# Two-block kernel on one core: the second tile's expert weights added by GpSimd into a cleared table, and a new order of the choice steps

## The chip, the cores and the metric

One core of a Trainium2 chip runs the whole program in one launch. The metric is device time in microseconds (us) for one execution. The engines are TensorE (PE), VectorE (DVE), ScalarE (ACT), GpSimd (Pool) and SyncE (SP), which issues most of the DMAs. TensorE runs at 2.4 GHz or, when the chip's gate holds it back, at 1.2 GHz; the profile gives the share granted as PEclk.

## What is computed

The reference is two transformer blocks on 512 tokens of width 1024 in float32. The first has gated delta-rule and sparse attention and an FFN; the second has gated linear attention, a state-space mixer and a PEER layer, which this case is about:

```python
q = (hb @ w_q).reshape(n, PEER_HEADS, 2, PEER_HALF)
s = jnp.einsum('nhid,hikd->nhik', q, sub_keys)
s_top, i_top = lax.top_k(s, PEER_TOPK)                 # 16 of 128, twice per head
cand = s_top[:, :, 0, :, None] + s_top[:, :, 1, None, :]
best, pos = lax.top_k(cand.reshape(n, PEER_HEADS, 256), PEER_TOPK)
w = jax.nn.softmax(best, axis=-1)
act = jax.nn.gelu(jnp.einsum('nhkd,nd->nhk', u, hb))   # u: rows of u_tab at idx
out = jnp.einsum('nhk,nhkd->nd', w * act, jnp.take(v_tab, idx, axis=0))
```

There are 8 heads, 16 picks per head (128 picks per token) and 16384 experts. An expert has a row in `u_tab` and one in `v_tab`.

## The kernel before

**Two ways to the experts.** The 512 tokens are four tiles of 128. For tile 0 the kernel fetches the 128 chosen rows of every token: a GpSimd indirect DMA brings row n of all tokens into a buffer `ub` (0.5 MB), and DVE multiplies it with the token (`gather_ve`, L3240, first 128 rows) or adds it, weighted, to `acc` (second 128 rows). For tiles 1 to 3 (ND = 384 tokens) it computes all 16384 experts densely: `u_pe` multiplies 128 tiles of `u_tab` with the tokens, ACT takes the gelu into `gst` and SP writes it to `gelu_spill`; later the v phase reads it back, multiplies it with a table of expert weights (mostly zeros) and multiplies the result with `v_tab`.

**The table of weights.** For tiles 1, 2 and 3 it is made in hot steps: a pick's expert is i * 128 + b, and for four tokens at a time DVE builds one-hot matrices `Bh` (L3027) and, with the weight, `Ah` (L3030), PE multiplies them (four matmuls of 128x128 per step), ACT copies the result into `stage` (L3011) and SP writes `stage` to `weight_spill` (`spill`, L3039), six halves of 4 MB in four DMAs of 1 MB each. One tile has 32 hot steps.

**The choice.** `top_ve(j)` makes tile j's list: for j of 2 and 3 sixteen `top16` on 128 values (for 0 and 1 these are done before this stage), then the sums of candidates, eight `top16` on 256 values, and seven passes over 2048 elements that turn places into indices, `sel`. `hot_*(j)` needs the list j, `gather_po` the list 0.

**The order.** Each engine's program is written by generators. `weave` takes a step of each in turn at given rates. `together((u_x, 1), (choose_x, CHOOSE))` weaves the dense u work (256 steps on each engine, four per 1 MB weight tile) with the choice, CHOOSE = 1.14 choice steps to one u-step. All engines use the same counts, so that their orders agree. `choose` runs top(0), top(1), then hot(1) with top(2) and 16 rows, hot(2) with top(3) and 16 rows, hot(3) with 16 rows, then 32 rows and the start of the v phase (`start_*`: SP fetches the first three pieces, DVE `weigh`s two, ACT makes the high half `ph`, DVE the low half `pl`). `top_idle` holds the place of a list on engines that have nothing to do in it, and must have as many steps.

**Weight tiles.** SP loads them into a ring of four. ACT makes the high half `wh` (L521), DVE the low half `wl` (L528), both with two buffers, and PE multiplies three times (high with high, low with high, high with low) at L573.

**Rows in flight.** `gather_po` issues row n after row n-2 is used, with two buffers, until row 48 (RT); from there with six buffers, four of which lie over `stage`.

**The first FFN** (`ffn_*`) begins with `arrive(.., 3)`; SP then loads `x1`, and DVE's `ffn_ve` waits for it, adds PE's results of the four `wout1` tiles to it and makes the `wl` of later tiles in between.

## Time and profile before

| | |
|---|---|
| median of 3 runs | 3211.97 us (3210.53 to 3214.05) |
| the profiled execution | 3215.74 us, span 3213.9 us |
| PE busy / DVE busy / ACT busy / Pool busy | 3068.6 / 2213.7 / 1152.6 / 418.7 us |
| mean granted TensorE clock | 0.967 |
| DMA | 571.10 MB, 178 GB/s over the span |
| of this: software queue (Pool's) | 134.23 MB in 36864 packets |
| chain that ended last | PE 79%, DVE 12%, DMA 4%, ACT 3% |

The span is the time from the first to the last instruction in the trace; the rest of the execution's time lies around it. A view of stretches gives the busy time of each engine between two times, with the number of instructions in brackets. In a view in order of time the bracket at the end of a row is the idle time before the instruction and who ended it. Busy spans of neighbouring instructions overlap a little, so a price is best taken from start to start. Busy PE time is not useful work as such: at half clock the same matmuls are busy twice as long.

### The profile page before, as it was taken

The numbers are of one execution on the slowest core, as the hardware profiler recorded it, in microseconds if no ns is written. First come the engines' busy times: TensorE is split into PE (matmuls) and PEld (weight loads), VectorE is DVE, ScalarE is ACT, GpSimd is POOL, SyncE is SP. The second block draws the span as 40 slices with busy tenths as digits, with TensorE's granted clock in tenths as the row PEclk, the third lists the DMA queues.
The fourth block names the chain that finished last, engine by engine and source line by source line (L and its number), as shares of the span: only waits on it lengthen the run. The fifth ranks groups of instructions, "written<-read, shape, count | busy, mean of one in ns | idle before, by whom it ended". The sixth has DMA issues, their size and how long they took to land.

```text
span 3213.9 us, 42988 instructions
## 1 busy us (share of the span) xinstructions
PE 3068.6 (95%) x17723; PEld 2809.3 (87%) x17723; DVE 2213.7 (69%) x3737; ACT 1152.6 (36%) x1569; POOL 418.7 (13%) x264
## 2 busy tenths in 40 slices
PE   7998998999999999999999999899999969999998
PEld 7887887878879889998877789899999969999998
DVE  6437875755644443567753568898998767899996
ACT  2224233222233442455543323344445522333332
POOL 0000000000000000000000000011111254565551
PEclk9889998999999998999999999899999989999999
DMA  5223112222232133212224414447777799999995
GB/s 230 88 111 146 40 53 105 75 94 100 79 125 89 67 109 133 79 53 81 86 91 164 170 66 144 154 168 233 258 235 260 268 378 352 403 402 401 402 399 216
DMA packets 215715, 571.10 MB, mean 178 GB/s; under 512 B 14289, under 2 KB 129489, under 8 KB 180065
## 3 DMA queue, kind: packets, MB, share of 16 engines
q1 hardware_dynamic: 176496, 426.14, 36.9%
q0 software_dynamic: 36864, 134.23, 10.9%
q10 hardware_dynamic: 2160, 7.99, 0.6%
q8 instruction: 140, 2.29, 0.3%
q14 instruction: 55, 0.44, 0.0%
HBM read 495.95 MB, written 72.35 MB: 177 GB/s over the span
## 4 chain that ended last, share of the span: by engine, by line
PE 79%; DVE 12%; DMA 4%; ACT 3%; SPq 1%; issue 1%; DVEq 0%; ACTq 0%
PE bank L573 71%; DMA wv<-weight_spill 3%; PE bank L1236 2%; DVE wl L528 2%; PE bank L637 2%; PE bank L2507 1%; PE bank L585 1%; PE bank L644 1%; DVE acc L148 1%; DVE Ah L3030 1%; PE bank L2516 1%; ACT wh L521 1%; PE bank L1501 0%; DVE sr L2859 0%; DMA cst<-in_consts 0%
## 5 line engine op out<-in xcount | busy, mean ns | idle before, releaser
L573 PE MATMUL bank<-hh,wh 128*128 128x512 f32 (+2 forms) x2512 | 925.1, 368 | 44.9 <-DVE wl L528 25.4
L573 PE MATMUL bank<-hl,wh 128*128 128x512 f32 (+2 forms) x2512 | 899.1, 358 | 0.0
L573 PE MATMUL bank<-hh,wl 128*128 128x512 f32 (+2 forms) x2512 | 894.1, 356 | 0.0
L528 DVE TENSOR_TENSOR wl<-ring,wh 128x2048 fp32r<-128x2048 f32 (+2 forms) x249 | 554.4, 2226 | 315.5 <-ACT wh L521 314.8
L521 ACT ACTIVATE wh<-ring 128x2048 fp32r<-128x2048 f32 (+2 forms) x249 | 463.7, 1862 | 781.2 <-PE bank L573 772.8
L573 PEld LDWEIGHTS bank<-hh,wh 128*128 128x128 f32 x2512 | 484.5, 193 | 101.5 <-DVE wl L528 28.4
L573 PEld LDWEIGHTS bank<-hl,wh 128*128 128x128 f32 x2512 | 484.8, 193 | 49.8 <-issue 6.0
L573 PEld LDWEIGHTS bank<-hh,wl 128*128 128x128 f32 x2512 | 484.3, 193 | 46.2
L3226 POOL DMA_INDIRECT ub<-in_urow,gsel x128 | 200.3, 1565 | 1452.8 <-DVE gsel L2957 885.7
L573 PE MATMUL bank<-ph,wh 128*128 128x384 f32 x1024 | 346.2, 338 | 22.0 <-DVE pl L3189 22.0
L573 PE MATMUL bank<-pl,wh 128*128 128x384 f32 x1024 | 345.3, 337 | 0.0
L573 PE MATMUL bank<-ph,wl 128*128 128x384 f32 x1024 | 345.2, 337 | 0.0
L3226 POOL DMA_INDIRECT ub<-in_vrow,gsel x128 | 216.9, 1695 | 148.2 <-DVE acc L148 115.1
L573 PEld LDWEIGHTS bank<-ph,wh 128*128 128x128 f32 x1024 | 193.5, 189 | 22.6 <-issue 20.8
L573 PEld LDWEIGHTS bank<-pl,wh 128*128 128x128 f32 x1024 | 193.5, 189 | 0.0
L573 PEld LDWEIGHTS bank<-ph,wl 128*128 128x128 f32 x1024 | 193.5, 189 | 0.0
L148 DVE SCALAR_TENSOR_TENSOR acc<-ub,gwt,acc 128x1024 f32<-128x1024 f32 x127 | 163.0, 1283 | 8.9 <-DVE acc L148 0.5
L3240 DVE SCALAR_TENSOR_TENSOR ub<-ub,hh_u 128x1024 f32<-128x1024 f32 x128 | 152.7, 1220 | 9.2 <-DMA ub<-in_urow,gsel 9.2
L573 PE MATMUL bank<-wh,hh 128*128 128x256 f32 (+2 forms) x520 | 154.3, 297 | 0.1
L573 PE MATMUL bank<-wh,hl 128*128 128x256 f32 (+2 forms) x520 | 150.8, 290 | 0.0
L573 PE MATMUL bank<-wl,hh 128*128 128x256 f32 (+2 forms) x520 | 150.8, 290 | 0.0
L1960 POOL TENSOR_TENSOR kdm<-kdm,km 128x16 f32<-128x16 f32 x4 | 1.3, 321 | 1131.9 <-ACT kdm L1927 1131.9
(515 smaller groups left out, 4456.0 us busy)
## 6 DMA issues: line engine op xcount, KB each, us to landing
ring<-in_v SPq DMA_DIRECT2D x68, 1024.0 KB, 16.2
ring<-in_u SPq DMA_DIRECT2D x64, 1024.0 KB, 5.6
ring<-in_ada SPq DMA_DIRECT2D x24, 1024.0 KB, 4.9
gelu_spill<-gst SPq DMA_DIRECT2D x128, 192.0 KB, 3.2
weight_spill<-stage SPq DMA_DIRECT2D x24, 1024.0 KB, 8.2
gv<-gelu_spill SPq DMA_DIRECT2D x64, 384.0 KB, 10.5
wv<-weight_spill SPq DMA_DIRECT2D x64, 384.0 KB, 14.5
ring<-in_wup SPq DMA_DIRECT2D x22, 1024.0 KB, 4.8
```

The lines of the kernel that those rows point to most:

```text
L148: return e.scalar_tensor_tensor(out=out, in0=a, scalar=x, in1=b, op0=op0, op1=op1)
L521: a.then_inc(a.e.activation(wh[q % 2][:, 0:n], ring[k % 4][:, 0:n], ACT.Copy), s("whi"))
L528: v.then_inc(v.e.tensor_tensor(wl[q % 2][:, 0:n], ring[k % 4][:, 0:n], wh[q % 2][:, 0:n].bitcast(F32), S_), s("parts"))
L573: ins = p.e.matmul(out, l, r, start=start and i == 0, stop=stop and i == len(pairs) - 1, skip_group_check=not check)
L585: return p.e.transpose(out, in_, ident[0:k, 0:k])
L637: ins = p.e.matmul(out[:, j:j + 1], sq[:, 128 * j:128 * j + 128], C["ones"][:, 0:1], start=start and j == 0, stop=stop, skip_group_check=True)
L644: ins = p.e.matmul(out[:, 128 * j:128 * j + 128], r[:, j:j + 1].to_broadcast([128, 128]), ident, start=j == 0, stop=True, skip_group_check ...
L1236: ins = p.e.matmul(ps[:, 128 * h:128 * h + 128], l, r, start=h == 0 and n_ == 0, stop=True, skip_group_check=True)
L2507: p.then_inc(p.e.matmul(bank[7][:, :], l, r, start=True, stop=True), s("ss_mm"))
L2516: p.then_inc(p.e.matmul(bank[6][:, :], CTm[:, q, 128 * j:128 * j + 128], SS[c % 2][:, :], start=q == 0, stop=q == 1), s("pi_mm"))
L3226: g.e.indirect_dma_start(ub[b][:, :], None, D["urow" if n < 128 else "vrow"], bass.IndirectOffsetOnAxis(gsel[:, 0, n % 128:n % 128 + 1], 0 ...
L3240: v.then_inc(v.e.scalar_tensor_tensor(out=u3, in0=u3, scalar=1.0, in1=hT, op0=M, op1=M, accum_out=dot[:, m:m + 1]), s("gd"))
```

## The change

Tile 1 no longer goes through hot steps. Its list yields `sidx`, the place of each of a token's 128 picks in a new table `weight_scatter` (64 x 2 x 128 x 128, 8 MB), and `swt`, the weights. GpSimd adds them there: 128 indirect DMAs with an add, each of 128 elements of 4 bytes, three after each gather from row 6 on. Every sixteenth waits until all earlier ones have landed. The table is cleared before by eight DMAs of 1 MB from a tile of zeros, at the start of the first FFN. `weight_spill` has four halves left, and `fetch` reads both tables.

The order of the choice is new too: rows stand beside top(1), top(2), hot(2) and hot(3), long steps are cut in two or have an empty step after them, and CHOOSE is 1.68. 88 rows, not 80, are used in the stage.

```diff
-    wd_ = nc.dram_tensor("weight_spill", (6, 64, 128, 2, 64), F32).ap()
+    wd_ = nc.dram_tensor("weight_spill", (4, 64, 128, 2, 64), F32).ap()
+    sw_ = nc.dram_tensor("weight_scatter", (64, 2, 128, 128), F32).ap()
...
         norm_ve(v, 2, x1, cc["lnmix"])
+        v.wait_ge(s("zw"), 128)
...
     def top_idle(j):
-        for _ in range((11 if j >= EARLY else 0) + 1 + 8 + 1 + 6 + 1):
+        for _ in range((19 if j >= EARLY else 0) + 1 + 16 + 1 + 12 + 1):
             yield
...
-        v.then_inc(tt(w3, w3, bc(red8[:, 1, :], 16), M), s("wsel"))
+        if j == 1:
+            v.then_inc(tt(swt.rearrange("p (h k) -> p h k", h=8), w3, bc(red8[:, 1, :], 16), M), s("wsel"))
+            v.then_inc(stt(v.e, sel[:, 0, :], sel[:, 1, :], 128.0, sel[:, 0, :], M, A_), s("ve"))
+            v.settle()
+            v.then_inc(ts(v.e, sidx, sel[:, 0, :], 128.0, M, stok[:, 0:1], A_), s("scr"))
+        else:
+            v.then_inc(tt(w3, w3, bc(red8[:, 1, :], 16), M), s("wsel"))
...
+    def cleared_po(g):
+        arrive(g, 3)
+        g.then_inc(g.e.memset(zeros[:, :], 0.0), s("zr"))
+        g.wait_ge(s("zr"), 1)
+        flat_w = sw_.rearrange("i x b t -> (i x b t)").rearrange("(p n f) -> p n f", p=128, f=2048)
+        for n in range(8):
+            g.e.dma_start(flat_w[:, n, :], zeros[:, :]).then_inc(s("zw").sem, 16)
+
+    def scatter_po(g, k):
+        cells = sw_.rearrange("i x b t -> (i x b t)").unsqueeze(1)
+        if k == 0:
+            g.wait_ge(s("zw"), 128)
+            g.wait_ge(s("wsel"), 2)
+            g.wait_ge(s("scr"), 1)
+        if k and k % 16 == 0:
+            g.wait_ge(s("scat"), 16 * k)
+        g.e.indirect_dma_start(cells, bass.IndirectOffsetOnAxis(sidx[:, k:k + 1], 0), swt[:, k:k + 1],
+                               None, compute_op=ALU.add).then_inc(s("scat").sem, 16)
...
-    ROWS = 0, 16, 32, 48, 80
+    ROWS = 0, 6, 22, 46, 70, 88
...
-        yield from top(1)
-        yield from weave((hot(1), 1), (top(2), 0.75), (rows(ROWS[0], ROWS[1]), 0.4))
-        yield from weave((hot(2), 1), (top(3), 0.75), (rows(ROWS[1], ROWS[2]), 0.4))
-        yield from weave((hot(3), 1), (rows(ROWS[2], ROWS[3]), 0.4))
-        yield from rows(ROWS[3], ROWS[4])
+        yield from weave((top(1), 1), (rows(ROWS[0], ROWS[1]), 0.2))
+        yield from weave((top(2), 1), (rows(ROWS[1], ROWS[2]), 0.33))
+        yield from weave((hot(2), 1), (top(3), 0.7), (rows(ROWS[2], ROWS[3]), 0.33))
+        yield from weave((hot(3), 1), (rows(ROWS[3], ROWS[4]), 0.33))
+        yield from rows(ROWS[4], ROWS[5])
         yield from start
...
-    CHOOSE = 1.14
+    CHOOSE = 1.68
...
         if i < 3:
-            y.wait_ge(s("ab_mm"), 96)
+            y.wait_ge(s("ab_mm"), 64)
+            y.wait_ge(s("scat"), 2048)
...
+        y.e.dma_start(ws[i % 3][:, :, :], sw_[i].rearrange("x b t -> b x t")).then_inc(s(f"gv{i % 3}").sem, 16)
...
-        g4 = gv[i % 3][:, :, :].rearrange("p x (b t) -> p x b t", b=6)
+        g3 = gv[i % 3][:, :, 0:128]
+        v.e.tensor_tensor(g3, g3, ws[i % 3][:, :, :], M)
+        g4 = gv[i % 3][:, :, 128:ND].rearrange("p x (b t) -> p x b t", b=4)
...
+            if n >= 6:
+                for k in range(3 * n - 18, min(3 * n - 15, 128)):
+                    scatter_po(g, k)
```

A hot step takes two choice steps on each engine now, a `top16` on 256 values two, and a `top16` on 128 values one (before, two of them shared a step); the counts in `top_idle`, `top_sc`, `hot_pe`, `hot_sc`, `hot_ve` and `hot_sy` follow.

Pool's queue before, whole from its last vector work on (`kdm` belongs to the gated linear attention):

```order
L1960 TENSOR_TENSOR kdm<-kdm,km 128x16 x4
L3226 DMA ub<-in_urow,gsel 128x1024 x128
L3226 DMA ub<-in_vrow,gsel 128x1024 x128
```

and after, from the clearing to the first scatters, and the end of the scatters:

```order
L2998 MEMSET zeros 128x2048
L3002 DMA weight_scatter<-zeros 128x2048 x8
L1966 ISA
L1966 TENSOR_TENSOR kdm<-kdm,km 128x16 x4
L3275 DMA ub<-in_urow,gsel 128x1024 x7
L3012 DMA weight_scatter<-cst 2097152x1 x3
L3275 DMA ub<-in_urow,gsel 128x1024
L3012 DMA weight_scatter<-cst 2097152x1 x3
L3275 DMA ub<-in_urow,gsel 128x1024
```

`cst` holds `sidx` and `swt`. From row 6 on each gather now has three scatters behind it, up to row 48.

SP's queue at the end of the stage before, where `gv` and `wv` are the first pieces of the v phase and `gst` the gelu results:

```order
L3138 DMA gelu_spill<-gst 128x384 x2
L508 DMA ring<-in_v 128x2048
L3138 DMA gelu_spill<-gst 128x384 x2
L3170 DMA gv<-gelu_spill 128x768
L3171 DMA wv<-weight_spill 128x6x128
```

and after:

```order
L3216 DMA gv<-gelu_spill 128x768
L3217 DMA wv<-weight_spill 128x4x128
L3219 DMA ws<-weight_scatter 128x2x128
L513 DMA ring<-in_v 128x2048
L3182 DMA gelu_spill<-gst 128x384 x2
L513 DMA ring<-in_v 128x2048
L3182 DMA gelu_spill<-gst 128x384 x2
```

The fetches stood behind the last gelu write; now eight gelu writes follow them.

DVE's queue at the same place before:

```order
L528 TENSOR_TENSOR wl<-ring,wh 128x2048
L3240 SCALAR_TENSOR_TENSOR ub,dot<-ub,hh_u 128x1024
L3178 TENSOR_TENSOR gv<-gv,wv 128x384 x4
L3189 TENSOR_TENSOR pl<-gv,ph 128x768 x2
```

and after:

```order
L533 TENSOR_TENSOR wl<-ring,wh 128x2048
L3224 TENSOR_TENSOR gv<-gv,ws 128x2x128
L3227 TENSOR_TENSOR gv<-gv,wv 128x256 x2
L3224 TENSOR_TENSOR gv<-gv,ws 128x2x128
L3227 TENSOR_TENSOR gv<-gv,wv 128x256 x2
L3238 TENSOR_TENSOR pl<-gv,ph 128x768
L533 TENSOR_TENSOR wl<-ring,wh 128x2048 x4
```

Four wl, two of them for the last two u tiles, now stand behind the first `weigh`.

## Rows read from the trace of the kernel before

**Rows 1.** Stretches: busy us (instructions), PE clock, DMA share, GB/s.

```profile
1955.00:2072.00 117.00, 100.07 (x527) 98.00 (x526) 108.42 (x240) 36.00 (x40) 3.96 (x2) 0.91 0.43 152
2072.00:2258.00 186.00, 181.46 (x1118) 180.54 (x1117) 170.87 (x419) 86.72 (x88) 27.76 (x16) 0.99 0.64 214
2258.00:2445.00 187.00, 183.24 (x1128) 182.60 (x1127) 172.77 (x420) 86.50 (x90) 25.95 (x16) 0.99 0.70 235
2445.00:2566.00 121.00, 120.88 (x784) 120.58 (x783) 95.16 (x203) 64.52 (x66) 21.29 (x19) 1.00 0.82 278
2566.00:2641.00 75.00, 58.98 (x312) 58.01 (x310) 48.73 (x68) 19.23 (x21) 42.63 (x29) 0.91 1.01 371
2641.00:2659.00 18.00, 0.35 (x1) 0.38 (x2) 9.07 (x13) 1.69 (x2) 6.18 (x5) 0.55 0.98 362
2659.00:3196.70 537.70, 536.19 (x3087) 535.90 (x3087) 475.99 (x487) 169.34 (x134) 289.46 (x170) 1.00 0.98 377
```

The engines stand in the order PE, PE's weight loads, DVE, ACT, Pool.

**Rows 2.** PE's waits, 1955 to 2660: total us, times, longest.

```profile
PE bank L573 <- DVE wl L528: 25.4, 10, 4.9
PE bank L573 <- ACT gst L3121: 9.3, 1, 9.3
```

**Rows 3.** ACT in order of time: gelus, without hot work and with it.

```profile
1976.59 0.49 ACT L3121 ACTIVATE gst<-bank 128x384 f32<-128x384 f32 x1 [1.88 <-PE bank L573]
...
1985.05 0.49 ACT L3121 ACTIVATE gst<-bank 128x384 f32<-128x384 f32 x1 [1.88 <-PE bank L573]
...
2178.78 0.49 ACT L3121 ACTIVATE gst<-bank 128x384 f32<-128x384 f32 x1 [1.00 <-PE bank L573]
...
2188.97 0.49 ACT L3121 ACTIVATE gst<-bank 128x384 f32<-128x384 f32 x1 [0.97 <-PE bank L573]
```

**Rows 4.** DVE in order of time: start, us, operation.

```profile
1976.70 0.43 DVE L2856 MAX8 hl_u<-s_ 128x8 f32<-128x256 f32 x1
...
1979.08 0.43 DVE L2856 MAX8 hl_u<-s_ 128x8 f32<-128x256 f32 x1
...
2185.27 0.67 DVE L3027 TENSOR_TENSOR Bh<-cst,hl_u 128x512 f32<-128x512 f32 x1
...
2186.89 1.22 DVE L3240 SCALAR_TENSOR_TENSOR ub<-ub,hh_u 128x1024 f32<-128x1024 f32 x1
...
2188.03 2.29 DVE L528 TENSOR_TENSOR wl<-ring,wh 128x2048 fp32r<-128x2048 f32 x1
2190.24 0.69 DVE L3027 TENSOR_TENSOR Bh<-cst,hl_u 128x512 f32<-128x512 f32 x1
...
2271.46 0.29 DVE L2856 MAX8 top<-s_ 128x8 f32<-128x128 f32 x1
...
2273.16 0.30 DVE L2856 MAX8 top<-s_ 128x8 f32<-128x128 f32 x1
```

**Rows 5.** The gathers (L3226) from 2060 to 2440: durations in ns, landing.

```profile
L3226 POOL DMA_INDIRECT ub<-in_urow,gsel x32: 936/1147/2748, 2072.3 to 2437.4; - x32
...
DMA to landing us min/median/max: 4.2/6.5/9.5
```

**Rows 6.** DVE and Pool in order of time at 2179.

```profile
2179.07 2.29 DVE L528 TENSOR_TENSOR wl<-ring,wh 128x2048 fp32r<-128x2048 f32 x1
...
2179.42 2.75 POOL L3226 DMA_INDIRECT ub<-in_urow,gsel  x1 [11.82 <-DVE ub L3240]
```

**Rows 7.** SP in order of time, two writes of 1 MB after hot(3).

```profile
2572.38 12.72 SPq L3039 DMA_DIRECT2D weight_spill<-stage  x2
```

**Rows 8.** The gelu writes (L3138): time to landing.

```profile
DMA to landing us min/median/max: 1.8/3.2/14.9
```

**Rows 9.** DVE in order of time: the first weigh of the v phase.

```profile
2654.30 1.03 DVE L3178 TENSOR_TENSOR gv<-gv,wv 128x384 f32<-128x384 f32 x2 [6.80 <-DMA wv<-weight_spill]
```

**Rows 10.** DVE in order of time: the first use of x1.

```profile
517.65 1.41 DVE L148 SCALAR_TENSOR_TENSOR x<-bank,modc,x 128x512 f32<-128x512 f32 x2 [10.85 <-DMA x<-in_xT]
```

**Rows 11.** The chain that ended last: PE's four wout1 tiles.

```profile
500.07 45.77 PE bank L573 x192
```

More of the change, by code:

```diff
@@ L371, in _build @@
         fcv = [sb(f"fcv{j}", [128, 512], F32, ar) for j in range(6)]
+        zeros = sb("zeros", [128, 2048], F32, ar)
     with ExitStack() as ar:
@@ L466, in _build @@
         dot = sb("dot", [128, 128], F32, ar)
+        stok = sb("stok", [128, 4], F32, ar)
+    sidx, swt = cst[:, 256:384].bitcast(U32), cst[:, 384:512]
     by_h8 = lambda ap: ap.rearrange("p (h k) -> p h k", h=8)
@@ L475, in _build @@
         gv = [sb(f"gv{j}", [128, 2, ND], F32, ar) for j in range(3)]
-        wv = [sb(f"wv{j}", [128, 6, 2, 64], F32, ar) for j in range(3)]
+        wv = [sb(f"wv{j}", [128, 4, 2, 64], F32, ar) for j in range(3)]
+        ws = [sb(f"ws{j}", [128, 2, 128], F32, ar) for j in range(3)]
         sb("past_choice", [128, 656], F32, ar)
@@ L2893, in top_sc @@
         w3 = sel[:, 2, :].rearrange("p (h k) -> p h k", h=8)
-        for _ in range((11 if j >= EARLY else 0) + 1 + 8 + 1 + 6):
+        for _ in range((19 if j >= EARLY else 0) + 1 + 16 + 1 + 12):
             yield
@@ L2909, in top_ve @@
                 top16(v, top[:, n, :], tix[:, n, :], s_[:, n, :], sr[:, 0:128])
-                if n % 2:
-                    yield
+                yield
         v.settle()
@@ L2924, in top_ve @@
             yield
+            yield
         for x, (op, by) in enumerate(((ALU.logical_shift_right, 4), (ALU.bitwise_and, 15))):
@@ L2935, in top_ve @@
             yield
+            yield
             v.settle()
@@ L2939, in top_ve @@
             yield
-            if j >= 2 and c == 0:
-                v.wait_ge(s("ijw_mm"), j - 1)
+            yield
+            if j == 3 and c == 0:
+                v.wait_ge(s("ijw_mm"), 1)
             v.settle()
@@ L2944, in top_ve @@
                        s("seld"))
+            yield
             yield
@@ L2969, in quads, with scatter_ve @@
     def quads(j):
-        return [(32 * j + q - 32, q) for q in range(32)]
-    WST = 192, 192
+        return [(32 * j + q - 64, q) for q in range(32)]
+    WST = 128, 128
+    def scatter_ve(v):
+        v.then_inc(v.e.tensor_tensor(sr[:, 0:128], ident, C["iota"], M), s("ve"))
+        v.settle()
+        v.then_inc(v.e.tensor_reduce(stok[:, 0:1], sr[:, 0:128], AX.X, A_), s("ve"))
+        v.settle()
+    def cleared_po(g):
[15 more added lines that the diff above has]
+                               None, compute_op=ALU.add).then_inc(s("scat").sem, 16)
     def hot_pe(p, j):
@@ L2997, in hot_pe @@
             yield
+            yield
         yield
@@ L3013, in hot_sc @@
             yield
+            yield
         yield
@@ L3018, in hot_ve @@
             yield
-        v.wait_ge(s("ijw_mm"), j)
-        if j >= 2:
-            v.wait_ge(s("ab"), 32 * j - 32)
+        v.wait_ge(s("ijw_mm"), j - 1)
+        if j == 3:
+            v.wait_ge(s("ab"), 32)
         v.then_inc(v.e.tensor_copy(ijw, bank[4][:, 0:384].rearrange("p (c k) -> p c k", c=3)), s("ijw"))
@@ L3027, in hot_ve @@
             v.e.tensor_tensor(Bh[t % 2][:, :, :], rep(C["iota"], 4), bc(ijw[:, 1, 4 * q:4 * q + 4], 128), ALU.is_equal)
+            yield
             for z in range(4):
@@ L3045, in hot_sy @@
             yield
-            if j > 1:
-                spill(y, 2 * j - 3, z)
+            if j == 3:
+                spill(y, 1, z)
         yield
@@ L3050, in hot_sy @@
             yield
-            if q in (16, 18, 20, 22):
-                spill(y, 2 * j - 2, (q - 16) // 2)
+            yield
+            if 16 <= q < 20:
+                spill(y, 2 * j - 4, q - 16)
         yield
-    ROWS = 0, 16, 32, 48, 80
+    ROWS = 0, 6, 22, 46, 70, 88
     def choose(turn, top, hot, rows, start):
@@ L3076, in rows_sy @@
         for n in range(n0, n1):
-            if n0 == ROWS[3] and n - n0 < 4:
-                spill(y, 5, n - n0)
+            if n0 == ROWS[-2] and n - n0 < 4:
+                spill(y, 3, n - n0)
             yield
@@ L3265, in start_sy @@
     def start_sy(y):
+        for _ in range(3):
+            yield
         for i in range(3):
             fetch(y, i)
-        yield from start_idle()
+        for _ in range(4):
+            yield
     def start_pe(p):
@@ L3497, in pool @@
         g = Line(e)
+        cleared_po(g)
         gprep_po(g)
```

23 lines of the change are left out of this document (12 added, 11 removed).

## The prediction, made before the changed kernel was run

> **What bounds the kernel now.** I read the stretches first [rows 1]. The change touches the last third: the expert stage from 1955 us, where TensorE (PE) makes 128 tiles of x times u while VectorE (DVE) chooses experts, and the v phase from 2659 us. From 2072 to 2566 PE is busy nearly all the time and DVE over 90% of it until 2445; in the v phase PE is full at granted clock 1.00. Three places have holes. From 1955 to 2072 two top lists stand one after the other on DVE: DVE is 93% busy and PE's clock is 0.91. From 2566 to 2641 the DMA engines are full (371 GB/s) and PE loses 16 us. From 2641 to 2659 PE stands still. Of PE's waits inside the stage 25.4 us end with a wl (the low half of a weight tile, made by DVE) and 9.3 us with a gelu write-out on ScalarE [rows 2]. So the stage has two near-equal bounds, PE and DVE, and its end a third, DMA.
>
> **Prices.** I call one yield of `u_pe` a u-step (12 matmuls; 256 in all, four per 1 MB weight tile). Two gelus four u-steps apart without hot work stand 8.46 us apart, so a u-step costs 2.115 us on PE. With two hot steps between them (four small matmuls each) it is 10.19, so a hot step costs PE (10.19 - 8.46) / 2 = 0.86 us [rows 3]. On DVE, from start to start [rows 4]: Bh with four Ah 1.62 us, a row 1.14, a wl 2.21, a top16 on 256 values 2.38, on 128 values 1.70. A top list is 8 x 2.38, seven passes of wl's shape (2.3 each, 16.1) and some 2 of small ones: 37.1 us; lists 2 and 3 add 16 x 1.70 and come to 64.3.
>
> **Part 1: one of three tiles leaves the hot path.** 32 hot steps go: PE loses 32 x 0.86 + 0.6 (three transposes) = 28 us, DVE 32 x 1.62 = 52, ScalarE 32 copies that hide anyway, SP eight writes of 1 MB. Only PE's and DVE's shares can shorten anything, and only where that engine is the bound.
>
> **Part 2: the new order.** I walk both orders with these prices. Choice yields are divided by CHOOSE to give u-steps, and a stage costs the larger of PE and DVE (DVE has a wl each fourth u-step).
> Before (CHOOSE 1.14): turn 7 u-steps with its transposes 18; two lists 34 yields, 29.8 u-steps, PE 63 against DVE 91; two weaves of 82 yields, 71.9 u-steps, PE 180 each (DVE 175); hot(3) 47.4 u-steps, PE 128; 32 rows 28.1 u-steps, PE 59. Sum 656 us, against 686 measured. Of the 30 left over 16 belong to the full DMA stretch and 14 to places where one engine waits for a single instruction.
> After (CHOOSE 1.68): turn 4.8 u-steps, 13. List 0, 31 yields, 18.5 u-steps: PE 39, DVE 47. List 1 with 6 rows, 22.0 u-steps: PE 47, DVE 57. List 2 with 16 rows, 66 yields, 39.3 u-steps: PE 83, DVE 64.3 + 18.2 + 21.7 = 104. Hot(2) with list 3 and 24 rows, 144 yields, 85.7 u-steps: PE 209, DVE 192. Hot(3) with 24 rows, 56 u-steps: PE 146, DVE 111. 18 rows, 10.7 u-steps: PE 23. Then 19 u-steps alone: 40. Sum 47 + 57 + 104 + 209 + 146 + 23 + 40 + 13 = 639. So the 28 us that PE is spared shrink to 17: with hot work gone from beside list 2 the first 80 u-steps are DVE's, and PE cannot go faster there. That is where I expect most of the saving to stay.
> Left-over waits: I keep 8 us of the 14 (only one weave still has both engines full). The DMA stretch I keep at 16: it has four spills, as before, in 4 choice yields that are now 2.4 u-steps and not 3.5 apart, with 18 rows of 0.5 MB and not 32. One such pair of writes held SP for 12.7 us [rows 7], and gelu write-outs queue behind it.
>
> **Part 3: scatter on GpSimd (Pool).** 128 indirect adds, three after each gather from row 6 on, so all are issued by row 48. No row shows such an add; the nearest is the gather's issue. It takes 0.94 us free, 1.15 in the median and 2.75 at worst [rows 5]; the long ones start under a wl and last until 0.8 us after it ends [rows 6], so a running DVE pass with two inputs holds Pool back. Four issues with gaps of 0.3 us and on average 0.4 of such holding are 6.6 us, and every sixteenth scatter waits until all have landed (some 0.5 us per row). That makes 7 us per row on Pool. Rows come every 6.5 us on DVE in list 2 (104 / 16) and every 8.7 in hot(2) (209 / 24). DVE takes rows in program order, so list 2 stretches by 16 x 0.5 = 8 us at most; I take 6. The list's scores are loaded after the list before is done, 2.4 u-steps ahead of their use and not 7: another 3. Two gathers in flight, each 6.5 us to landing [rows 5], allow a row per 4 us and don't bind. Lower bound of this part 0 (a Pool with no holding needs 5.5 us per row); the upper one is the second rival.
> The Trainium skill ("DMA: Bandwidth & Descriptors", Specifications) says that a transfer under 512 B becomes a read-modify-write. Its section "Two DMAs through the same engine are not ordered" says that descriptors start in order but are pipelined. By the first each of these 4-byte writes is dear, by the second they overlap and the sum stands. No row of before decides it; the third rival says what it would do.
>
> **Part 4: clearing the table.** At the start of the first FFN Pool writes 8 MB of zeros, just when SP loads x1. DVE waits 10.9 us for x1 already [rows 10], and behind it on DVE's queue stands the wl for the third of four wout tiles, each 11.4 us on PE [rows 11]. Sharing the DMA engines delays x1 by 4 to 8 us; under 2 us of that are slack. PE then waits 2 to 6 us and runs some microseconds at half clock: I take 5 (0 to 12).
>
> **Part 5: the hand-over to v.** Before, the fetches go out after the last gelu write, their data end a wait of 6.8 us on DVE [rows 9], and PE is still for 18 us, then starts v at half clock (2 more). Now the first fetch stands 16 u-steps before the end. Its cost moves: DVE comes to `weigh` two choice yields after the fetch is issued, while before the data were there 13 us after the stage had ended [rows 1, 9]. Behind weigh on DVE stands the wl of the last but one u tile, and on ScalarE `upper` stands ahead of its wh. A tile's slack is 8.5 us less 4.1 for wh and wl. So PE waits about 5 us and loses 3 to the clock: 8 (0 to 16). Gain 20 - 8 = 12.
> `weigh` is three passes of 256 for two of 384; eight rows fewer (8 x 1.14 us) pay for that on DVE, which is 89% busy in v. PE is the bound there and nothing else changes: 0. ScalarE's exp and the two small DVE steps for the indices cost under 1 us.
>
> **Sum.** Stage and hand-over: before 686 + 18 + 2 = 706. After: 639 + 8 + 16 + 6 + 3 + 8 = 680. With the clearing 685: 21 to 22 us less. The profiled execution took 3215.7 us (span 3213.9), 3.8 above the median of 3212; from it I get 3194, as a median 3190.
>
> **Rivals.** *Everything is covered* (chance 0.15): Pool keeps up, the zeros hide, weigh finds its data, spills thin out: 3190 - 9 - 5 - 8 = 3168. For it: Pool is idle most of the stage. Against: each cover is thin.
> *GpSimd becomes the bound of list 2* (0.15): an add needs twice a gather's issue, or is held by DVE each time, so a row takes 8.5 us of Pool against 6.5. Stretch 16 x 2 = 32 where I took 6 (and 0 in hot(2), at 8.7): 3215, no change that can be told.
> *The adds are slow in memory* (0.12), the slower side. 128 elements over 16 DMA engines are 8 each. If each must land before the next starts, at the shortest landing of a small write, 1.8 us [rows 8], one scatter takes 14 us; if they overlap, it is well under 1. Gathers stand behind them in the same queue. It decides from 2.2 us per scatter (6.5 / 3). At 4 us a row takes 12: 16 x 5.5 + 24 x 3.3 = 167 more, 3355.
> *The DMA jam grows* (0.08): spills and rows come 1.5 times as densely, the hole at the end of hot(3) goes from 16 to 45 us: 3220. Against: fewer bytes in all.
>
> **Chances.** Forecast 0.50, with its own range 3172 to 3205. A measurement of this kernel tells 0.2% (6.4 us) from no change. Faster: 0.50 less 0.02, and 0.15, makes 0.63; same 0.17; slower 0.20. The range 3160 to 3225 leaves out the slow adds and a little beneath: 0.15 to 0.2.
>
> **What would show it.** Right: between hot(2)'s start and hot(3)'s end PE is full and its clock 1.0; before that DVE over 95% busy with PE's clock near 0.9, for some 220 us from 1955; no hole at the start of v but one of 5 us some 30 us earlier; x1's wait longer by 4 to 8 us. Wrong: rows on DVE waiting for gathers in list 2 by more than 10 us in all (Pool or slow adds); landings of gathers much over 6.5 us while scatters run; SP held over 20 us after hot(3).

## The result: slower by 1.3%, and the profile after

The changed kernel takes 3254.1 us in the median (3250.4 to 3258.9, 5 runs). The ratio to the kernel before is 1.0127, 95% interval 1.0112 to 1.0142. I had forecast 3190: the sign is wrong, and the time lies outside the range. The profiled execution took 3252.7 us (span 3250.9).

To compare kernels whose orders differ I cut each trace at marks that all have: the first gelu, the `Exp` that ScalarE does at the end of each list, the last `stage` copy (end of hot(3)), the last gelu, the end. Stretches in us:

| | turn, list 0 | list 1 | list 2 | hot(2), list 3 | hot(3) | up to the last gelu | from there to the end | span |
|---|---|---|---|---|---|---|---|---|
| before | 56.4 | 47.2 | 184.1 (with hot(1)) | 181.1 | 127.7 | 82.5 | 573.9 | 3213.9 |
| forecast | - | 57 | 104 + 9 | 209 | 146 | 23 + 40 + 16 + 8 | 554 | 3192 |
| after | 56.3 | 58.4 | 135.7 | 232.5 | 164.5 | 92.8 | 548.1 | 3250.9 |

Three stretches are too long, by 23, 24 and 18 us; the rest is within 6 us. The 8 us of left-over waits in the forecast belong to no single stretch and are not in the row. Each stretch comes from one profiled execution: where two kernels have the same orders up to a mark, their stretches differ by up to 2 us (before and b_clear below), once by 6 (hot(3) in c_both and c_jam), so a few us in one stretch are not a finding. The same stretches of after, cut near these marks (columns as in [rows 1]):

```profile
1955.00:2077.00 122.00, 108.02 (x605) 105.06 (x604) 117.00 (x250) 37.54 (x42) 13.64 (x7) 0.99 0.57 193
2077.00:2213.00 136.00, 95.62 (x464) 92.71 (x462) 103.09 (x253) 30.19 (x33) 110.55 (x64) 0.87 0.63 167
2213.00:2445.00 232.00, 212.88 (x1264) 208.96 (x1265) 187.22 (x436) 96.08 (x99) 166.58 (x95) 0.97 0.74 206
2445.00:2610.00 165.00, 147.96 (x910) 145.15 (x908) 110.50 (x225) 73.98 (x76) 44.22 (x36) 0.97 0.77 246
2610.00:2703.00 93.00, 70.14 (x390) 69.48 (x390) 44.53 (x56) 23.59 (x27) 31.86 (x23) 0.89 0.92 332
2703.00:3233.00 530.00, 530.00 (x3065) 530.00 (x3065) 471.87 (x531) 168.45 (x134) 273.00 (x162) 1.00 0.98 375
```

In list 2 (second line) DVE is busy 103 of 136 us, so it isn't the bound that I had made it: my walk had DVE full for 104. Pool is busy 110.6 us with 64 issues; with the gaps of 0.3 us between them (18.6 us), 7.6 us of waiting for the first indices and 4.1 us of waiting for landings, it is full. In hot(2) and hot(3) (third and fourth line) PE, which was to be full there, lacks 19 and 17 us, DVE is at 81% and 67%, and Pool is busy 167 of 232 us and 44 of 165: no engine is full. PE's waits in the whole stage, where before there were two kinds [rows 2], and a third at the hand-over to v, shown further down:

```profile
PE bank L578 <- DVE wl L533: 70.0, 18, 22.4
PE bank L578 <- DVE Ah L3073: 34.9, 21, 5.5
PE bank L590 <- DVE sel L2968: 8.4, 1, 8.4
```

The waits for `Ah` are new, and so is one of 8.4 us in which PE's transposes for hot(2) wait for list 2 (`sel`). The waits for wl were 25.4 us before.

**Pool in list 2**, a piece in order of time:

```profile
2154.97 1.00 POOL L3275 DMA_INDIRECT ub<-in_urow,gsel  x1 [0.30 <-issue]
2156.27 2.98 POOL L3012 DMA_INDIRECT weight_scatter<-cst  x1 [0.30 <-issue]
2159.56 1.56 POOL L3012 DMA_INDIRECT weight_scatter<-cst  x1 [0.30 <-issue]
2161.43 1.55 POOL L3012 DMA_INDIRECT weight_scatter<-cst  x1 [0.30 <-issue]
2163.28 1.00 POOL L3275 DMA_INDIRECT ub<-in_urow,gsel  x1 [0.30 <-issue]
2164.59 2.74 POOL L3012 DMA_INDIRECT weight_scatter<-cst  x1 [0.30 <-issue]
2167.63 1.56 POOL L3012 DMA_INDIRECT weight_scatter<-cst  x1 [0.30 <-issue]
2170.85 1.55 POOL L3012 DMA_INDIRECT weight_scatter<-cst  x1 [1.66 <-DMA weight_scatter<-cst]
2172.70 1.00 POOL L3275 DMA_INDIRECT ub<-in_urow,gsel  x1 [0.30 <-issue]
```

From gather to gather 8.3 and 9.4 us pass (8.4 in the mean over the 16 rows of list 2), and Pool does little but issue. An undisturbed scatter is 1.56 us of issue against a gather's 1.00. Once per row one is about 1.3 us longer, as the gathers were before that a wl held back [rows 6]: the two long ones here start under a wl on DVE (2155.53 to 2157.80 and 2163.60 to 2165.87) and end 1.5 us after it. Only in the last turn does Pool wait for a landing: this is the wait that stands ahead of every sixteenth scatter. In list 2 these waits are 4.1 us in all, while DVE's rows wait for gathers:

```profile
DVE ub L3292 <- DMA ub<-in_urow,gsel: 26.9, 9, 6.9
```

The time from issue to landing of the scatters in that stretch (shortest, median, longest):

```profile
DMA to landing us min/median/max: 2.9/4.0/7.1
```

**hot(2)**, where PE waits for `Ah`. First ScalarE in order of time:

```profile
2296.15 1.92 ACT L526 ACTIVATE wh<-ring 128x2048 fp32r<-128x2048 f32 x1 [1.04 <-PE bank L578]
```

DVE at the same place:

```profile
2294.68 0.69 DVE L3069 TENSOR_TENSOR Bh<-cst,hl_u 128x512 f32<-128x512 f32 x1
...
2298.10 2.29 DVE L533 TENSOR_TENSOR wl<-ring,wh 128x2048 fp32r<-128x2048 f32 x1 [1.15 <-ACT wh L526]
2300.30 1.12 DVE L3073 TENSOR_SCALAR Ah<-cst,hl_u 128x128 f32<-128x128 f32 x4
```

And PE:

```profile
2301.57 1.13 PE L578 MATMUL bank<-Bh,Ah 128*128 128x128 f32 x8 [3.41 <-DVE Ah L3073]
```

The chain reads: PE leaves a weight tile; only then can ScalarE write the next `wh` into the buffer that came free (1.92 us); DVE, in order, stands at wl for it and then makes wl (2.29); `Ah` of a step whose `Bh` was long made stands behind (1.12); PE has meanwhile reached the hot step's matmuls and waits. From PE's release to `Ah` that is 1.9 + 2.3 + 1.1 = 5.3 us, and for the last 3.4 of them PE stood still.

**Behind hot(3)** SP is held as before [rows 7]. SP in order of time:

```profile
2625.28 12.87 SPq L3082 DMA_DIRECT2D weight_spill<-stage  x2
2638.19 11.81 SPq L513 DMA_DIRECT2D ring<-in_u  x1
```

Two gelu writes follow only at 2650.58, and ScalarE, DVE and PE wait in turn. PE stands still once for long, until

```profile
2665.49 0.69 PE L578 MATMUL bank<-hh,wh 128*128 128x384 f32 x1 [22.37 <-DVE wl L533]
```

### The profile page after: what moved, and what is told of

Same layout as the page of the kernel before. It is cut to its first block and busy times, and to the rows that moved or that the text cites. A ratio compares the mean times of both kernels' runs of the same rounds, so it can differ in the third digit from the quotient of the medians.

```text
span 3250.9 us, 42506 instructions
## 1 busy us (share of the span) xinstructions
PE 3054.3 (94%) x17464; PEld 2786.2 (86%) x17464; DVE 2167.0 (67%) x3644; ACT 1120.4 (34%) x1537; POOL 647.5 (20%) x401
## 5 line engine op out<-in xcount | busy, mean ns | idle before, releaser
L3275 POOL DMA_INDIRECT ub<-in_urow,gsel x128 | 178.2, 1392 | 1192.5 <-DVE gsel L2972 886.0
L3012 POOL DMA_INDIRECT weight_scatter<-cst x128 | 245.3, 1916 | 59.4 <-issue 36.9
## 6 DMA issues: line engine op xcount, KB each, us to landing
ring<-in_v SPq DMA_DIRECT2D x68, 1024.0 KB, 10.2
```

The source lines that it names most:

```text
L3012: g.e.indirect_dma_start(cells, bass.IndirectOffsetOnAxis(sidx[:, k:k + 1], 0), swt[:, k:k + 1], None, compute_op=ALU.add).then_inc(s("sca ...
L3275: g.e.indirect_dma_start(ub[b][:, :], None, D["urow" if n < 128 else "vrow"], bass.IndirectOffsetOnAxis(gsel[:, 0, n % 128:n % 128 + 1], 0 ...
```

## Theories

**A.** An adding scatter's issue takes Pool 1.56 us, so a row takes 8.5 us of Pool where DVE asks for one each 6.5; list 2 is Pool's. (My second rival.) **Against it:** the adds are slow in memory or crowd the DMA queue (my third rival).

**B.** Cutting the hot step in two, `Bh` in one choice step and `Ah` in the next, took DVE's lead over PE. Before, `Ah` was made two hot yields ahead of its use, and a hot yield was 2.15 / 1.14 = 1.9 u-steps; so 3.8 u-steps, 8 us; in hot(3), where no list stood beside the hot steps, it was 2 x 1.4 / 1.14 = 2.5 u-steps, 5.2 us. Now it is one yield of (1 + 0.7 + 0.33) / 1.68 = 1.2 u-steps in hot(2), 2.6 us, and 0.8 in hot(3), 1.7 us, less than the 5.3 of the chain above. (All leads are counted at 2.1 us per u-step, without the hot work in between, so they are a little too short.) **Against it:** DVE is simply late by its load.

The two lie in different stretches, so each kernel below is read by stretch. All ratios are to the kernel before; its median in the three sets of runs was 3214.7, 3211.5 and 3214.2.

## First set: each theory alone

**a_unsplit.** One part undone:

```diff
             v.e.tensor_tensor(Bh[t % 2][:, :, :], rep(C["iota"], 4), bc(ijw[:, 1, 4 * q:4 * q + 4], 128), ALU.is_equal)
-            yield
             for z in range(4):
...
             v.then_inc(ins, s("ab"))
             yield
+            yield
```

> One part of the change undone: in a hot step DVE makes Bh and Ah in one choice step again, with two empty steps behind, where the changed kernel makes Bh in one and Ah in the next. So Ah of a step is made two choice yields of the hot work before TensorE multiplies it, not one. Theory B (the cut step took DVE's lead over TensorE, and the two now wait for each other in hot(2) and hot(3)): PE's 34.9 us of waits for Ah fall below 10, DVE's 77 us of waits for ScalarE's wh below 40, the stretch from hot(2)'s ijw copy to hot(3)'s end (404 us) loses 20 to 35 us, list 2 stays at 136; in all 3254 - 27 = 3227 (3219 to 3236). Rival R1 (DVE and Pool are simply full there, the waits for Ah are their late work): the waits change their name, to wl, and the time stays within 5 us of 3254.

**a_lead.** The same, and the consumers one step later:

```diff
         p.then_inc(ins, s("ijw_mm"))
         yield
         yield
         yield
+        yield
...
     def hot_sc(a, j):
-        for _ in range(5):
+        for _ in range(6):
...
-            if 16 <= q < 20:
-                spill(y, 2 * j - 4, q - 16)
+            if 17 <= q < 21:
+                spill(y, 2 * j - 4, q - 17)
```

(the last `yield` of `hot_pe` and `hot_sc` goes, so that the count stays.)

> As a_unsplit, and TensorE's four small matmuls, ScalarE's copy and SP's writes of a hot step stand one choice step later, so that Ah is made three yields ahead of its use and DVE may overwrite the buffers one yield after TensorE has read them, not two. Theory B: another 0 to 8 us less than a_unsplit, 3223 (3212 to 3234). Rival R1: within 5 us of 3254. Rival R2 (what matters is DVE being blocked behind TensorE, at the Bh that waits for the matmuls two steps before): slower than a_unsplit, by 5 us and more.

**a_two.** Fewer scatters per row, none left out:

```diff
-                for k in range(3 * n - 18, min(3 * n - 15, 128)):
+                for k in range(2 * n - 12, min(2 * n - 10, 128)):
```

> Two scatters behind each gather from row 6 on, not three, so the last is issued with row 69 and not 48. Nothing is left out. Theory A (Pool's issue of a scatter, 1.9 us in the mean, makes Pool the bound of list 2, where a row takes it 8.7 us and DVE asks for one each 6.5): Pool takes 1.13 + 2 x 1.92 + 3 x 0.3 = 5.9 us per row, under 6.5, list 2 goes from 136 to 107-115 us, the rows' waits on DVE in all (41.5 us) fall below 15; hot(2), where DVE asks each 8.7, is little changed; 3254 - 24 = 3230 (3224 to 3238). Rival A1 (the scatters cost in memory or on the DMA queue, by their number in flight): the number is the same, gathers still wait behind them, 3254 to 3262. Rival A2 (list 2 is long for the order's sake, DVE's own work): within 5 us of 3254.

**a_noscat.** Without the scatters:

```diff
-            if n >= 6:
-                for k in range(3 * n - 18, min(3 * n - 15, 128)):
-                    scatter_po(g, k)
...
-            y.wait_ge(s("scat"), 2048)
```

> The 128 scatters and the wait for them before the v phase are left out (the experts of tile 1 then have weight zero); clearing, indices, weights and the reads of the table stay. It bounds what the scatters cost in all. Theory A: list 2 at 105 to 112 us, 24 to 31 less, and at most 5 more in hot(2) from Pool's free port; 3254 - 28 = 3226 (3219 to 3234), so a_two is within 6 us of it. Rival A2: within 5 us of 3254. If scatters also hold the rows in hot(2) (rival A3): below 3219.

**Measured.**

| | median, us | ratio, 95% | list 2 | hot(2) | hot(3) | up to the last gelu |
|---|---|---|---|---|---|---|
| after | 3254.1 | 1.0127 (1.0112-1.0142) | 135.7 | 232.5 | 164.5 | 92.8 |
| a_unsplit | 3224.3 | 1.0027 (1.0017-1.0036) | 136.2 | 213.4 | 157.2 | 93.6 |
| a_lead | 3220.3 | 1.0019 (1.0010-1.0029) | 132.9 | 214.4 | 152.5 | 91.4 |
| a_two | 3226.6 | 1.0035 (1.0021-1.0050) | 108.8 | 235.1 | 161.4 | 95.4 |
| a_noscat | 3224.5 | 1.0029 (1.0018-1.0041) | 108.2 | 235.6 | 158.6 | 92.4 |

The two causes come apart. The edits of the lead leave list 2 nearly alone (within 3 us) and take 26 and 30 us from hot(2) and hot(3) together; those of the scatters take 27 us from list 2 and leave hot(2) alone (3 us more). a_two issues all 128 adds and is as quick as the kernel without any (2 us apart, inside the intervals): beyond their issue the adds cost nothing that can be measured here, and their issue costs only where Pool is the bound. That ends my third rival. The rows' waits in list 2 of a_two:

```profile
DVE ub L3292 <- DMA ub<-in_urow,gsel: 0.8, 1, 0.8
```

PE's waits for `Ah` from 2210 to 2580 in a_unsplit:

```profile
PE bank L578 <- DVE Ah L3072: 14.0, 8, 7.5
```

and in a_lead:

```profile
PE bank L578 <- DVE Ah L3071: 7.4, 3, 2.9
```

They fell from 34.9 to 14.0 and 7.4; I had expected under 10 for the first. DVE's waits for `wh`, 77 us in after, are 53 in a_unsplit, where I had expected under 40. DVE's load is the same in all three, so the rival that it was late by its load falls. The time came out as expected (3224 for 3227, 3220 for 3223; a_two 3227 for 3230, a_noscat 3225 for 3226). Whether a_lead's further 4 us are real can't be told (the intervals overlap).

## Second set: do they add, and the other terms of the sum

**c_both** is a_lead and a_two together.

> The edits of a_lead and of a_two together: Bh and Ah in one choice step, TensorE's small matmuls a step later, two scatters behind each gather. If the two causes lie in different stretches (list 2 for the scatters, hot(2) and hot(3) for the lead) the gains add: 34 + 27.5 = 61, 3254 - 61 = 3193 (3187 to 3200), 0.6% under the kernel before; list 2 near 107 us, hot(2) near 214, hot(3) near 152. Rival: they draw on one slack (Pool, now issuing scatters in hot(2) and hot(3) too, is late there once DVE is quick, with 24 rows in 214 us or 8.9 us each against 5.9 to 7 us of Pool): half of the smaller gain is lost, 3205 to 3210.

**c_jam** spaces the last writes of `stage`:

```diff
-            if n0 == ROWS[-2] and n - n0 < 4:
-                spill(y, 3, n - n0)
+            if n0 == ROWS[-2] and (n - n0) % 4 == 0 and n - n0 < 16:
+                spill(y, 3, (n - n0) // 4)
```

> c_both, and the last four 1 MB writes of stage to weight_spill stand beside rows 70, 74, 78 and 82 instead of 70 to 73. In a_lead PE stood still once for 21.7 us there (DVE's wl behind ScalarE's gst behind the gelu write-outs, which stood behind these writes on SP). Theory J1 (SP is held by bunched writes of small pieces): the hole falls below 8 us, 3193 - 14 = 3179 (3172 to 3187). Rival J2 (the DMA engines are full there by the sum of their bytes, some 335 GB/s, in whatever order): the hole only moves, within 4 us of c_both. Rival J3: the later writes delay the first fetch of the v phase by up to 5 us, and with it weigh: slower than c_both by 0 to 5.

**c_hand** holds the start of v back:

```diff
         yield from rows(ROWS[4], ROWS[5])
+        for _ in range(27):
+            yield
         yield from start
```

> c_both with 27 empty choice steps (16 u-steps) on every engine ahead of the start of the v phase, so that its fetches go out about where the kernel before had them, behind the last gelu write. Theory H (the 25.7 us by which the stretch after the last gelu became shorter come from the earlier fetch): 22 to 28 us slower than c_both, near 3218, with a PE hole of some 18 us before v. Rival H2 (they come from something else at the end, as from fewer rows or bytes in the v phase): within 8 us of c_both.

**b_clear** is the kernel before with one edit of the change alone:

```diff
+        zeros = sb("zeros", [128, 2048], F32, ar)
...
+        v.wait_ge(s("zw"), 128)
         end_ve(v)
...
         g = Line(e)
+        cleared_po(g)
         gprep_po(g)
```

> The kernel before, and only the clearing of the new table added to it at the start of the first FFN (memset, eight DMAs of 1 MB, a wait for them at the end of the FFN); nothing reads the table. Read from the trace of the changed kernel, the clearing costs 1.5 us (DVE's wait for x1 12.8 us, from 10.9; the expert stage starts 1.5 us later): 3212 + 1.5, a ratio of 1.0005 (0.9995 to 1.0015) to the kernel before. The prediction had 5 us: 1.0016.

**Measured.**

| | median, us | ratio, 95% | list 2 | hot(2) | hot(3) | up to the last gelu | from there |
|---|---|---|---|---|---|---|---|
| c_both | 3186.4 | 0.9922 (0.9904-0.9939) | 108.6 | 208.4 | 146.5 | 95.8 | 547.3 |
| c_jam | 3188.0 | 0.9918 (0.9901-0.9935) | 109.1 | 208.3 | 152.4 | 93.4 | 547.3 |
| c_hand | 3196.9 | 0.9942 (0.9924-0.9961) | 108.8 | 208.4 | 146.9 | 95.5 | 562.6 |
| b_clear | 3212.4 | 0.9996 (0.9987-1.0006) | | | | | 572.4 |

**c_both**: the gains add. In ratios 1.08% and 0.92% make 2.00%, measured 2.05%. The kernel is faster than before by 0.8%, and its stretches are near those of my walk (list 2 109 for 113, hot(2) 208 for 209, hot(3) 146.5 for 146). Its stretches, from the end of list 1 on:

```profile
2075.00:2184.00 109.00, 90.02 (x466) 87.06 (x464) 102.39 (x255) 30.11 (x32) 87.20 (x50) 0.94 0.72 214
2184.00:2393.00 209.00, 207.60 (x1269) 207.60 (x1270) 187.46 (x438) 97.04 (x100) 128.05 (x71) 0.99 0.75 228
2393.00:2539.00 146.00, 143.45 (x908) 141.92 (x907) 110.23 (x224) 72.36 (x73) 118.24 (x67) 1.00 0.88 269
2539.00:2635.00 96.00, 72.24 (x387) 71.25 (x386) 45.01 (x56) 23.50 (x26) 42.80 (x30) 0.88 0.93 331
```

In list 2 DVE is busy 102 of 109 us, in hot(2) PE 207.6 of 209: the two engines that the forecast had as bounds. The granted clock in list 2 is 0.94, for 0.87 in after, where PE stood still more.

Together the edits take 42 us from hot(2) and hot(3), a_lead alone 30. A part of the other 12 is Pool's: once DVE is quick, three scatters per row fill Pool in hot(2) too. There Pool waited for DVE to be done with a row, in a_lead,

```profile
POOL ub L3274 <- DVE ub L3291: 1.4, 1, 1.4
```

and in c_both

```profile
POOL ub L3274 <- DVE ub L3291: 65.7, 20, 7.1
```

(30.9 us in after). The half of it that lies in hot(3), 6 us, is no more than c_both and c_jam differ there.

**c_jam**: the same within its interval. The stretch behind hot(3) is 2 us shorter than in c_both, and hot(3), which the edit doesn't touch, is 6 us longer in this profile. PE's waits for wl behind hot(3) are 18.5 us in all for 23.8. Spacing the writes is not the remedy (theory J1 falls).

**c_hand**: 10.5 us slower in the median, 15.3 in the last stretch of the profiles, neither the 22 to 28 of theory H nor the 8 and less of H2. PE's wait ahead of v is

```profile
PE bank L578 <- DVE pl L3239: 12.6, 1, 12.6
```

and before, in the same view,

```profile
PE bank L573 <- DVE pl L3189: 20.5, 1, 20.5
```

So of the 26.6 us by which c_both's last stretch is under that of before (573.9), 15.3 come from the early fetch. From the last gelu to the first matmul of v 18.6 us passed before and 10.7 in c_hand: another 8. The last 3.4 are in v itself (555.3 us to the end before, 551.9 here).

Why the hand-over of c_hand is itself shorter than that of before can be read from the traces. The first fetches of `gv` took, from issue to landing (shortest, median, longest), before

```profile
DMA to landing us min/median/max: 7.4/13.3/14.3
```

and in c_hand

```profile
DMA to landing us min/median/max: 3.0/3.8/5.2
```

Before, the DMA engines were full while these fetches ran, and in c_hand they were not (before, then c_hand):

```profile
2641.00:2655.00 14.00, 0.00 (x0) 0.00 (x0) 6.39 (x9) 0.00 (x0) 6.18 (x5) 0.57 1.04 403
2634.00:2645.00 11.00, 0.51 (x2) 0.54 (x3) 5.88 (x9) 1.95 (x3) 0.00 (x0) 0.52 0.73 232
```

Pool issued rows in the first of these stretches and none in the second. So the 8 us go with shorter landings on freer DMA engines. No run here parts the rows from the other traffic.

**b_clear**: no cost that can be measured. DVE did wait longer for its input at the start of the FFN:

```profile
  DMA x<-in_xT: 12.9, 1
```

2.0 us more than before [rows 10], yet PE's wait behind it grew only from 2.6 to 2.8 us, and the expert stage began at 1960.8 us, 1961.0 before: slack took it.

## Third set: why B works, what the add costs, and what is left

**a_shift** has only the consumers later, and leaves `Bh` and `Ah` cut (the edit of a_lead without that of a_unsplit).

> The changed kernel with Bh and Ah still in two choice steps, and only TensorE's small matmuls, ScalarE's copy and SP's writes of a hot step one choice step later: Ah stands two choice yields ahead of its use, as in a_unsplit (which took 30 us off), but a wl may still stand between Bh and Ah on DVE. Theory B (the number of yields between Ah and its use is what counts): 3227 (3220 to 3233), hot(2) and hot(3) stretches near 213 and 157 us, as in a_unsplit. Rival B2 (what counts is that a wl that waits for ScalarE can stand between Bh and Ah): 3245 to 3256, stretches near 232 and 165. Between them: both.

**c_160** is c_both with

```diff
-    CHOOSE = 1.68
+    CHOOSE = 1.6
```

> c_both with CHOOSE 1.6 and not 1.68, so that each choice step has 5% more u work beside it. Theory P (in the first 134 choice steps after the turn, lists 0 to 2, DVE is the bound and TensorE is short of work: 56, 58 and 109 us there, TensorE at 90 of 109 in list 2): the same lists take DVE the same time and 4 more u-steps lie beside them, hot(2) and hot(3) are TensorE's and grow by 5%, the tail shrinks by all that was moved: 4 x 2.1 less some wl time of 2 us, 3186 - 6 = 3180 (3174 to 3186). Rival P2 (the later start of the v phase, 10 u-steps before the end of the dense work and not 18, exposes the hand-over): the gain is given back, 3186 to 3196, with a hole of PE before v.

**d_plain** is the changed kernel with writes that don't add:

```diff
-                               None, compute_op=ALU.add)
+                               None)
```

> The changed kernel with indirect DMAs that write and don't add (a token that has picked an expert twice, by two heads, keeps one of the two weights). Number, size and places of the transfers are the same. Theory W (an indirect DMA whose places are single elements in memory costs Pool 1.56 us of issue, add or not): issue 1.5 to 1.6 us, list 2 near 136 us, 3254 (3248 to 3260). Rival W2 (the add doubles the issue): a write takes 0.94 us as a gather does, Pool needs 6.6 us per row, list 2 near 110 us, 3254 - 26 = 3228.

**c_early4** is c_both without the last four writes, and with four of the same size at an earlier place:

```diff
-            if n0 == ROWS[-2] and n - n0 < 4:
-                spill(y, 3, n - n0)
...
+            if j == 3 and 21 <= q < 25:
+                z = q - 21
+                y.e.dma_start(wd_[3, 16 * z:16 * z + 16].rearrange("s i x t -> i s (x t)"),
+                              stage[0][:, 32 * z:32 * z + 32, :].rearrange("p (s x) t -> p s (x t)", x=2)
+                              ).then_inc(s("wst0").sem, 16)
```

> c_both, and the last four 1 MB writes of stage, beside the rows behind hot(3), are gone; in their place the half before is written twice, during hot(3) (so the weights of the last 16 hot steps are those of the 16 before). It keeps the bytes and takes four of them out of the last 96 us. Theory J2 (that stretch is bound by the sum of its bytes, 331 GB/s over 96 us, 4 of some 32 MB): the stretch behind the last stage copy falls from 96 to 84-88 us, and hot(3), with a DMA share of 0.88 before, grows by 0 to 6; 3186 - 6 = 3180 (3174 to 3186). Rival J1 (not bytes, but work of DVE and ScalarE behind the turn of buffers): within 3 us of c_both.

**Measured.**

| | median, us | ratio, 95% | list 2 | hot(2) | hot(3) | up to the last gelu | from there |
|---|---|---|---|---|---|---|---|
| a_shift | 3223.7 | 1.0022 (1.0002-1.0042) | 135.1 | 215.4 | 156.5 | 93.1 | 547.3 |
| d_plain | 3233.1 | 1.0053 (1.0036-1.0069) | 116.9 | 235.8 | 162.9 | 95.0 | 547.3 |
| c_160 | 3175.8 | 0.9885 (0.9868-0.9901) | 111.1 | 213.3 | 151.8 | 70.9 | 552.7 |
| c_early4 | 3177.9 | 0.9884 (0.9867-0.9900) | 108.3 | 208.8 | 150.1 | 84.4 | 548.8 |

**a_shift** does what a_unsplit does (215 and 157 us against 213 and 157), although a wl can still stand between `Bh` and `Ah`. So it is the distance between `Ah` and its use that counts, and not that the step is in one piece (B2 falls). Theory B stands: the time is 3224, where it gave 3227.

**d_plain** settles the price. The adding scatters of after in the first 113 us of list 2 (duration in ns: shortest, median, longest; first and last start):

```profile
L3012 POOL DMA_INDIRECT weight_scatter<-cst x39: 1552/1577/3529, 2079.7 to 2186.9; - x39
```

and the software queue of the whole kernel after (packets, MB, share of the 16 DMA engines):

```profile
q0 software_dynamic: 56448, 142.70, 13.1%
```

The plain scatters of d_plain, in the same view:

```profile
L3012 POOL DMA_INDIRECT weight_scatter<-cst x49: 966/992/2969, 2077.5 to 2189.0; - x49
```

and its software queue:

```profile
q0 software_dynamic: 42112, 142.70, 11.8%
```

A plain scatter is issued in 0.97 us, as a gather. The add makes it 1.55, and 14336 packets more, 112 for each DMA, for the same bytes. The extra packets are small ones, 14335 of them under 512 B. Over all queues, after has

```profile
DMA packets 219809, 571.15 MB, mean 176 GB/s; under 512 B 33744, under 2 KB 132560, under 8 KB 183136
```

and d_plain

```profile
DMA packets 205474, 571.15 MB, mean 177 GB/s; under 512 B 19409, under 2 KB 118225, under 8 KB 168801
```

W falls, W2 stands, with 3233 us for its 3228. List 2 is 116.9 us, not 110: Pool's four issues (1.31 us each in the mean), their gaps and 8.8 us of waits for landings in 16 rows make 7.0 us per row, a little over the 6.5 that DVE grants.

**c_early4**: the stretch behind hot(3) is 11 us shorter and hot(3) 4 longer; the median is 8.5 us below c_both. (The two were measured in different sets. By their ratios to the kernel before they are 0.38% apart, 12 us.) The bytes are enough to account for it (J2): the stretch held 0.93 of the DMA engines' time in c_both, and 4 MB at its 331 GB/s are 12.7 us. One thing is not parted from the bytes. The edit also takes the four writes out of SP's queue ahead of the gelu writes, and ScalarE's waits for the gelu writes went with them, from 43.3 us in c_both to 3.5. c_jam only shows that spacing the writes, with bytes and number kept, saves nothing. (The profiled execution of c_early4 is no shorter than that of c_both only because the expert stage began 6 us later in it.)

**c_160**: 10.6 us below c_both (12 by the ratios), where 6 were expected; 3.6 of the 10.2 us between the profiles lie ahead of the stage. The lists take 2.5 us more, hot(2) and hot(3) 10 more, the stretch behind them 25 less and v 5 more. The price of the later fetch (P2) is there, a wait of PE for `pl`, but small. PE's waits from 2600 to 2700 us:

```profile
PE bank L578 <- DVE wl L533: 14.6, 1, 14.6
PE bank L578 <- DVE pl L3237: 3.6, 1, 3.6
```

c_160 leaves nothing out, and at 3175.8 us it is 1.15% faster than the kernel before: the quickest of the full kernels here.

## Why the prediction was wrong, step by step

**Part 3, "Four issues with gaps of 0.3 us and on average 0.4 of such holding are 6.6 us": wrong, a term mis-sized.** Gaps and holding were right (0.3, and about 1.3 once per row, so 0.33 an issue). The issue was not: I took the gather's 0.94 for the add, which takes 1.56. Three of them are 1.9 us more. That makes 8.5 per row for 6.6, against DVE's 6.5; the waits for landings were 0.3 per row where I had 0.5, and 8.4 us were measured from gather to gather. List 2 came to 135.7 us where I had 113. The second rival said this with the same 8.5 and 32 us; I gave it 0.15. Its 3215 us was too low all the same, because the next step was missing from it too. The row that I priced from was an indirect DMA with no arithmetic, and d_plain shows that just this was the difference.

**Part 2, "a stage costs the larger of PE and DVE" with "left-over waits: I keep 8 us of the 14": wrong, a wait overlooked.** Both engines' loads were right: hot(2) 209 and hot(3) 146 are what c_both takes. But a stage costs the larger load only if neither waits for the other in turn. I counted what the cut hot steps do to the number of steps and not how far ahead of its use `Ah` then stands: 8 us before (5.2 in hot(3)), 2.6 and 1.7 after, against a chain of 5.3. hot(2) and hot(3) took 42 us more than forecast. a_lead takes back 30 of them; the other 12 go only together with a_two, and at least a part of these is Pool full in hot(2), where Part 3 had 0. No rival had the missing lead. The 8 us of left-over waits that I kept don't show in c_both, whose hot(2) and hot(3) are at the larger load. It could have been seen beforehand: the steps at which `hot_ve` makes `Ah` and `hot_pe` uses it stand in the code, and that PE's list of waits before names wl and not `Ah` [rows 2] spoke for a lead that was there, not for none being needed.

**Part 4, 5 us for clearing: too high.** The wait for the input grew by 2 us and the time by nothing (0.9996).

**Part 5, the hand-over: right in direction, wrong in two sizes, and with one cause missing.** The hole before v vanished. The last stretch is 26 us shorter, not 20. Of this c_hand gives the early fetch 15; some 8 go with shorter landings at the hand-over, which the prediction didn't have, and some 3 lie in v, where it had 0. The cost of 8 for `weigh` did not come: in c_both DVE waits for the fetched pieces

```profile
DVE gv L3223 <- DMA ws<-weight_scatter: 7.8, 2, 5.4
```

and PE doesn't wait at all from 2600 to 2700 us; DVE's lead covered it.

**The full DMA stretch, 16 us: too low.** PE lost one hole of 22.4 us, and 23.8 in three in c_both. With no cost for `weigh` the sums are near each other (87 forecast, 92.8 and 95.8 measured).

**List 1: right.** 57 against 58.4. Part 1's prices are right too as far as c_both shows, since its hot(2) and hot(3) take what these prices give.

**The sum.** The stretches of the two failed steps are 23 and 42 us over, 65 together, and the time is 64 over the forecast: the smaller misses nearly cancel.

**The signs.** DVE's rows waited 26.9 us for gathers in list 2, over the 10 that I had named for a late Pool or slow adds. The gathers there landed in 4.6 us in the median, not over 6.5, which spoke for Pool and not for memory. SP was held for 24.7 us on end behind hot(3), over the 20 that I had named.

**The rivals.** *Slow adds*: a scatter is issued every 1.9 us and lands after 4.0 in the median, so they overlap, and all waits for landings make 4.1 us in list 2. The shortest landing of a scatter was 2.9 us; the 1.8 that I took was that of a 192 KB write. The Trainium skill ("DMA: Bandwidth & Descriptors", section "Two DMAs through the same engine are not ordered") says that descriptors start in order and are pipelined, which agrees with this trace. The rule of the Trainium skill on transfers under 512 B (the same page, section "Specifications": they are read-modify-writes) is not seen as a cost in time here: a_two, with 128 scatters of 4-byte elements, and a_noscat, with none, are 2 us apart. *A growing jam*: PE lost 23 us behind hot(3), 7 more than before and not 29.

With the two failed steps mended (c_both) the kernel takes 3186 us, 4 under the forecast. The walk held in list 2, hot(2) and hot(3). That the sum is so near is in part luck: the stretch up to the last gelu is 9 us longer than forecast, the one behind it 7 shorter, and the 5 us for clearing and the 8 of left-over waits did not come. The forecast failed on one price that was not in the trace and one dependency that was in the code.

## What to carry to other kernels

A step that is cut or delayed in a woven order changes how far ahead of its reader each result is made; compute that lead in microseconds on both sides and hold it against the longest in-order chain that can get between (here `wh`, wl, `Ah`: 5.3 us), before summing loads. When the trace has no row for an operation that will sit 128 times on one engine, take the nearest row and also twice its value, and see at which value that engine becomes the bound: here the margin was 0.5 us per row on the wrong side already. Fewer issues per row in the tight stretch and more in the loose ones cost nothing here: a_two spreads the same 128 adds to row 69 and is as quick as a_noscat.
